# A two-layer flow-matching backbone on one core: one transfer issued earlier, eight half products left out, the end of a projection dealt out anew, and head sums as four small products

## The reference

```
h   = rms_norm(x) * (1 + scale) + shift          # latent and context tokens
u   = h @ w_in                                   # keys, values, decay and rate latents, receptances, gate
z   = token_shift(u)                             # three taps along the tokens
w   = exp(-exp(-softplus(-(w0 + tanh(wd) @ w2)) - 0.5));  a = sigmoid(a0 + ad @ a2)
kk  = k * k_k / max(norm_per_head(k * k_k), 1e-12)
for each direction, head, token:                 # state S is 64 x 64 per head, 16 heads
    S = S * w - (S kk) (kk a)^T + v k^T;   y = S r
bonus = sum_over_the_64_channels_of_a_head(r * k_dir * r_k) * v
o   = group_norm(y_0 + y_1) * gn_w + gn_b + bonus_0 + bonus_1
out = x + gate_l * ((o * silu(gate)) @ w_out)
```

## Time and profile before

| | us |
|---|---|
| timed runs, median (lowest to highest) | 4983.27 (4974.59 to 4983.56) |
| the profiled execution, its own time | 4975.48 |
| its span, first to last instruction | 4973.5 |
| end of the projection of layer 1 | 3051 |
| recurrence | 3051 to 4672 |
| output stage | 4672 to 4973 |

### The profile page before, as it was taken

One profiled execution on the slowest core, in us unless ns is written; L12 is line 12 of the kernel. 1 busy time (PEld: TensorE's weight loads), 2 busy tenths in 40 slices (PEclk: granted clock), 3 DMA queues, 4 the chain that ended last, 5 costly groups with the idle time before them and its releaser, 6 DMA issues. The chain is left out here.

```text
span 4973.5 us, 120092 instructions
## 1 busy us (share of the span) xinstructions
PE 4543.6 (91%) x48286; PEld 2711.2 (55%) x48286; DVE 2692.2 (54%) x4764; ACT 1699.0 (34%) x4125; POOL 1377.6 (28%) x2884
## 2 busy tenths in 40 slices
PE   6999996999999999899999996888988998989599
PEld 4666663333333333454444444777877877778444
DVE  2444443655666663222144444666766676666487
ACT  1222221444444443033122222444544555445232
POOL 1111111332322331000000001555555555555232
PEclk8999997999999999899999998999999999999799
DMA  5222223000000002632322334777776777776685
GB/s 215 94 88 95 85 77 127 4 25 24 25 25 24 25 6 100 224 137 102 117 67 80 95 99 135 177 192 177 179 179 175 180 187 188 178 181 162 175 261 173
DMA packets 994713, 603.89 MB, mean 121 GB/s; under 512 B 699045, under 2 KB 939173, under 8 KB 980136
## 3 DMA queue, kind: packets, MB, share of 16 engines
q1 hardware_dynamic: 907690, 574.11, 39.9%
q10 hardware_dynamic: 86528, 22.82, 2.2%
HBM read 390.44 MB, written 206.32 MB: 120 GB/s over the span
## 5 line engine op out<-in xcount | busy, mean ns | idle before, releaser
L934 PE MATMUL at_bS<-at_qT,at_kT 97*64 97x512 f32 (+1 forms) x2368 | 607.1, 598 | 15.1 <-ACT at_pT L1032 14.5
L1673 PE MATMUL p_bU<-keep_hT,p_slab 128*128 128x512 f32 (+1 forms) x1504 | 596.9, 554 | 13.5 <-DMA p_slab<-in_o_w_in_dram 7.4
L1069 DVE TENSOR_REDUCE at_mx<-at_bM 128x1 f32<-128x512 f32 (+1 forms) x656 | 394.0, 627 | 353.8 <-PE at_bM L899 352.8
L2321 PE MATMUL rw_bank<-keep_rw_hg,rw_slab 128*128 128x256 f32 x2048 | 493.0, 395 | 45.7 <-DMA keep_rw_hg<-scratch_hT 45.7
L1032 ACT ACTIVATE at_pT<-at_bS 128x512 f32<-128x512 f32 (+1 forms) x592 | 342.4, 591 | 398.3 <-PE at_bS L934 379.0
L2321 PEld LDWEIGHTS rw_bank<-keep_rw_hg,rw_slab 128*128 128x128 f32 x2048 | 390.8, 196 | 108.5 <-DMA keep_rw_hg<-scratch_hT 47.9
L1673 PEld LDWEIGHTS p_bU<-keep_hT,p_slab 128*128 128x128 f32 x1504 | 283.9, 191 | 297.8 <-issue 281.8
L2114 POOL TENSOR_TENSOR rw_g_at<-rw_g_at,rw_g_prod 64x14 f32<-64x14 f32 (+6 forms) x1008 | 328.4, 326 | 79.0
L856 POOL TENSOR_TENSOR at_sum_pool<-at_sum_pool,at_pT 128x512 f32<-128x512 f32 x192 | 243.9, 1270 | 372.3 <-ACT at_pT L1032 354.9
L2112 POOL TENSOR_TENSOR rw_g_prod<-rw_g_at 64x14 f32<-64x14 f32 (+6 forms) x1008 | 315.8, 313 | 79.1
L934 PEld LDWEIGHTS at_bS<-at_qT,at_kT 97*64 97x64 f32 x2368 | 155.4, 137 | 279.8 <-issue 187.6
(11 more groups left out here) (288 smaller groups left out, 9463.1 us busy)
## 6 DMA issues: line engine op xcount, KB each, us to landing
keep_rw_hg<-scratch_hT SPq DMA_DIRECT2D x64, 1024.0 KB
keep_wide<-scratch_heads SPq DMA_DIRECT2D x144, 384.0 KB, 4.3
keep_gate<-scratch_inverses SPq DMA_DIRECT2D x576, 64.0 KB
scratch_bq<-keep_wide SPq DMA_DIRECT2D x144, 128.0 KB, 2.5
scratch_products<-rw_NB SPq DMA_DIRECT2D x288, 64.0 KB
rw_Vt<-scratch_vt SPq DMA_DIRECT2D x144, 128.0 KB, 2.6
scratch_y<-rw_ysb ACTq DMA_DIRECT2D x288, 64.0 KB, 3.2
scratch_heads<-p_z SPq DMA_DIRECT2D x17, 1024.0 KB, 4.9
```

The source lines that it names most:

```text
L934: last = pe.matmul(bS[rows, g % 3, 0:nq * P], kT[:, s, k * P + VH * x:k * P + VH * x + VH], qT[:, s, q0 * P:(q0 + nq) * P], start=True, st ...
L1069: nc.vector.tensor_reduce(mx[:, j, piece:piece + 1], bM[:, (FIRST_ITEM[b] + i) % 2, 0:n], AX.X, ALU.max).then_inc(max_red, 1)
L1673: last = pe.matmul(bU[:, n % 4, 0:w], slab[:, i, k, :], hT[:, k, tok:tok + w], start=(k == 0), stop=(k == KD - 1))
L2321: last = pe.matmul(DENSE[:, GT * half:GT * (half + 1)], slab[:, half, q, :], hg[:, x.slot, q, :], start=(q == 0 and half == 0), stop=(q == ...
```

## The change

Four parts, all in layer 1.

1. *Recurrence, SP.* `dense_before(n)` moves up: it stood behind `keep_inverses` and `gather`, and now stands ahead of both, right behind `keep_products`. At the start of the stage, `low_rank` of the first body reads its latents from a free slot of the prefetch buffer (`zin[:, 1, i, 3]`), which the projection stage fills with two small loads; it no longer waits for `rw_lora`. The second body waits for two of the three parts.
2. *Recurrence, TensorE.* In the last pass `dense(x, 0)` returns after its waits: 8 bodies times 8 products fall away.
3. *End of the projection.* In the last pair the values' outer taps stand ahead of `p_kk` on VectorE; two of the five copies of the last values and two of their four stores go to ScalarE; and in every pair the stores of the values of the pair before stand ahead of the `p_kk` stores.
4. *Output stage.* A head sum is four products of 64 x 64 by 512 columns, one on each quarter of the array, in place of two of 128 x 128. For two of the quarters the bonus products of the second half of the head pairs are loaded with the two heads of a pair swapped, which takes three transfers in place of one for each direction. `turn` now stands ahead of `head_sums` on TensorE and takes over its waits, and at the start of the stage GpSimd's first power stands ahead of its first sum.

```
@@ projection, SP, every pair
                         if i == 0:
+                            if not (isinstance(p, int) and p == 0):
+                                store_values(p - 1)
                             sp.wait_ge(kk_done, p + 1)
                             store(heads[:, 1, :], kk, kk_st)
                             sp.dma_start(heads[:, 2, 0:CTX], kk[:, 0:CTX]).then_inc(kk_st, 16)
-                            if not (isinstance(p, int) and p == 0):
-                                store_values(p - 1)
@@ projection, SP, end
+                for i in range(2):
+                    sp.dma_start(zin[:, 1, i, 3], W["lora"][i, :, 0:GT]).then_inc(keep["rw_wl_l"], 16)
...
                 pair(PAIRS - 1, False)
-                store_values(PAIRS - 1)
+                sp.wait_ge(vt_out, NS * (PAIRS - 1) + 3)
+                sp.wait_ge(vt_last, 2)
+                for h in range(2):
+                    sp.dma_start(turned_rows(PAIRS - 1, 0, h), vt[0:HP, :, HP * h:HP * h + HP]).then_inc(vt_st, 16)
@@ projection, ACT, end
+                a.wait_ge(vt_st, 16 * 4 * (PAIRS - 1))
+                for x in (1, 3):
+                    a.wait_ge(vt_mm, NS * (PAIRS - 1) + x + 1)
+                    nc.scalar.copy(vt[:, 4 * x:4 * x + 4, :].rearrange("p q c -> p (q c)"), bS[:, x, :]).then_inc(vt_last, 1)
+                a.wait_ge(vt_last, 2)
+                a.wait_ge(vt_out, NS * (PAIRS - 1) + 3)
+                for h in range(2):
+                    a.dma_start(turned_rows(PAIRS - 1, 1, h), vt[HP:P, :, HP * h:HP * h + HP]).then_inc(vt_st, 16)
@@ projection, DVE
+                    if p == PAIRS - 1:
+                        shift_taps(0, 0, slice(p + KD, p + KD + 1), 4 + 2 * p, links + 3)
                     v.wait_ge(dchain, links + 3)
...
-                    shift_taps(0, 0, slice(p + KD, p + KD + 1), 4 + 2 * p, links + 3)
-                for x in range(NS):
+                    if p < PAIRS - 1:
+                        shift_taps(0, 0, slice(p + KD, p + KD + 1), 4 + 2 * p, links + 3)
+                for x in range(0, NS, 2):
                     values_out(PAIRS - 1, x)
@@ recurrence, SP
                     keep_products(n.on(3), 1)
+                    dense_before(n)
                     keep_inverses(n.on(2))
                     gather(n.on(3))
-                    dense_before(n)
                     spread(n.on(2))
@@ recurrence, PE
-                    if m.n < 3:
-                        pe.wait_ge(lora_l[m.n], 16)
+                    for part in ((), (0, 1), (2,))[m.n] if m.n < 3 else ():
+                        pe.wait_ge(lora_l[part], 16)
...
-                                                 lora[rows, i, span(tokens(m, d), GT)], start=True, stop=True, skip_group_check=True)
+                                                 lora[rows, i, span(tokens(m, d), GT)] if m.n else zin[rows, 1, i, 3, :], start=True, stop=True, skip_group_check=True)
...
                         pe.wait_ge(dn_out, x.t)
+                        if not x.queries:
+                            return
@@ output, SP
-                        sp.dma_start(bin_[:, s, d], W["bq"][d, :, rows(t, CTX)].rearrange("(k p) t -> p k t", p=P)).then_inc(b_l[s], 16)
+                        sp.dma_start(bin_[:, s, d, 0:4], W["bq"][d, 0:4 * P, rows(t, CTX)].rearrange("(k p) t -> p k t", p=P)).then_inc(b_l[s], 16)
+                        for h in range(2):
+                            other = W["bq"][d, 4 * P:, rows(t, CTX)].rearrange("(k h c) t -> h c k t", h=2, c=HP)[1 - h]
+                            sp.dma_start(bin_[HP * h:HP * h + HP, s, d, 4:8], other).then_inc(b_l[s], 16)
@@ output, POOL, start of the stage
-                bonus(0, 0)
                 rstd(0)
+                bonus(0, 0)
                 rstd(1)
@@ output, PE
                 def turn(t, s):
+                    pe.wait_ge(bs_done, t + 1)
+                    pe.wait_ge(bv_done, t)
                     pe.wait_ge(yn_done, t + 1)
...
-                def head_sums(t):
-                    pe.wait_ge(bs_done, t + 1)
-                    pe.wait_ge(bv_done, t)
+                def head_sums():
                     for j in range(2):
-                        last = pe.matmul(bB[:, j, :], same[:], bsum[:, 4 * j:4 * j + 4, :].rearrange("p k t -> p (k t)"), start=True, stop=True)
+                        for h in range(2):
+                            rows_in, rows_out = (slice(HP * x, HP * x + HP) for x in (h, h ^ j))
+                            last = pe.matmul(bB[rows_out, j, :], same[rows_in, rows_in], bsum[rows_in, 4 * j:4 * j + 4, :].rearrange("p k t -> p (k t)"),
+                                             start=True, stop=True, skip_group_check=True)
                     last.then_inc(hs_mm, 1)
...
                     if next1:
-                        head_sums(t + 1)
                         turn(t + 1, 1 - s)
+                        head_sums()
                     pe.wait_ge(o_done, t + 1)
```

24 lines of the change are left out of this document (13 added, 11 removed).

## The result

| | before | changed |
|---|---|---|
| timed runs, median (lowest to highest), us | 4978.93 (4970.96 to 4983.56) | 5102.57 (5096.81 to 5109.36) |
| the profiled execution, its span | 4973.5 | 5095.0 |
| last reciprocal's end to the start of the recurrence | 29.5 | 25.1 |
| recurrence | 1621.4 | 1752.3 |
| output stage | 300.9 | 298.5 |

The ratio is 1.0251, with a 95% interval of 1.0229 to 1.0272: 124 us slower, where 4937 us, 42 under this median, was forecast. The two stages at the ends became shorter, by 4.4 and 2.4 us. The recurrence lost 131 us.

The account below looks back on a forecast made before the run. TensorE, busy 91% of the span, was taken to bound the kernel. Gains of 4.2 + 4 + 28 + 2 + 4.4 = 42.6 us gave 4932.9 from the profiled 4975.5, 4940.7 from the median; forecast 4937, range 4912 to 4966.

Parts of the forecast that it names:

- End of the projection: Projection's last pair: earlier transposes, copies and stores, some on a second queue, gain 4.2 us, bounds 2 and 6.
- Start of the recurrence: Recurrence's first bodies: early latents worth 0, since the slice's transfer limits; earlier slice issue gains 4 us later.
- The 4 us for the fourth body: Recurrence's fourth body: earlier slice issue wins 4 us of 3.81 waited plus 2.36 of longer products, bounds 0 and 6.
- The hoist in the other bodies: Recurrence bodies without new slabs: 1 MB ahead of inverses' store, gather and eight loads costs 0, as GpSimd has slack.
- Cost 0: Recurrence bodies without new slabs: the earlier slice costs nothing, GpSimd being busy only 28% of the span.
- the fourth rival: Recurrence: small transfers behind 1 MB land late, TensorE waits in every body, 68 us lost, 5000 us; chance 0.05.
- my "slower" rival: Same as the fourth rival: small transfers come late in every recurrence body, 5000 us; chance 0.05.
- The hoist at the boundaries: Recurrence's seven pass boundaries: slabs issued 3.6 us earlier win 4 us each, 28 in all, bounds 14 and 42.
- Last pass: Recurrence's last pass without half 0 of the dense products: 2 us gain, bounds 11 of gain and 9 of loss.
- Output stage: Output stage: head sums 1.09 us for 1.88, loop period stays; gain 4.4 us, mostly at the start, bounds 2 and 16.
- R3: Recurrence boundaries: the hoist does nothing because slabs also wait for their buffer; only the ends gain, 4969 us; chance 0.06.

Follow-up runs that it names:

- x1: Kernel before with only the hoist: `dense_before` ahead of `keep_inverses` and `gather` in every body; ratio 1.0239.
- x9: Kernel before with GpSimd's inversion made longer by computing seven of its products twice; ratio 1.0106.
- x11: Changed kernel with only the parts at the ends, the slice loaded behind `spread` for the body after next; ratio 1.0010 to the kernel before.
- x3: Changed kernel with `dense_before` early only in the seven bodies that need new slabs, at its old place elsewhere; ratio 1.0008 to the kernel before.
- x18: x1 with the gather and the inverses' store issued by GpSimd on its own queue; ratio 1.0222 to the kernel before.
- x10: Kernel before with four of the fourteen steps of GpSimd's inversion left out; ratio 0.9998.
- x14: x11 with four of the fourteen steps of GpSimd's inversion left out as well; ratio 0.9986 to the kernel before.
- x6: Kernel before with half 0 of the dense products not issued in the last pass; ratio 1.0006.
- x4: Kernel before with `dense_before` between `keep_inverses` and `gather`, so only the gather is behind the slice; ratio 1.0113.
- x15: Kernel before with the gather issued by GpSimd on its queue, just ahead of its inversion; ratio 1.0059.

## Why the prediction was wrong, point by point

- *End of the projection*, 4.2 us: right. From the last reciprocal's end to the next stage 29.4 to 29.7 us in thirteen traces with the old end, 25.1 to 25.5 in seven with the new one.
- *Start of the recurrence*, the latents: right. From the start of the stage to the first dense product there are 14.4 to 14.7 us in nineteen traces, with the early load and without it, and 17.2 in the changed kernel's own. The 4 us for the fourth body did not come: in x1 the wait for its slice is gone (3.81 before), but the next of the rows that stand once a body comes 81.2 us into the stage, where it came after 80.9.
- *The hoist in the other bodies, "Cost 0"*: this is the step that failed, with 119 us. I had priced it by GpSimd's slack, read from its 28% of the whole span. Over the six passes it is busy 644.33 of 1175.05 us, 55%, and its 7.2 us of waiting in each body were mostly no slack: 2.5 us more of work on GpSimd cost 53 us (x9). But this is not where the loss came from. I then argued against the fourth rival that the eight loads "lie behind the same bytes before and after". The loads do, but what they wait for, the inverses' store, had been ahead of the 1 MB and went behind it; its landing rose from 4.0 to 7.6 us. The loads began 8.8 us after the products' stores in place of 5.2. That is my "slower" rival, with 0.05: its mechanism, small transfers that come late for TensorE in each body, was right. Its price of 68 us was too small, because it gave the loads 5 us in hand: they came 3.7 us later, and each undisturbed body grew by 2.1 us (21.31 to 23.40), which over its 57 bodies is 119. So what they had in hand was less than 3.7 us. The waits of `far_p`, 67.9 us, are only a part of the loss, and TensorE's products took longer as well.
- *The hoist at the boundaries*, 28 us: wrong too. The wait for the slice did fall, from 32.4 to 9.0 us, but x11 takes all of it away and x3 keeps the hoist to these bodies, and neither is faster. In the changed kernel the body of group 0 takes 28.4 us, where 23 was forecast. A wait on TensorE was read as time that would be won. The three bodies around a boundary take 67.3 us before, 68.6 in x11 and 70.1 in x3, whichever of them waits.
- *Last pass*, 2 us of gain: not confirmed, its sign open; the products filled gaps, as argued.
- *Output stage*, 4.4 us: 2.4. The head sums took 1.09 us and `m_yn` still 3.37, and the loop kept its period to 0.1 us, as forecast. The gain is at the start: the first `m_yn` stands 14.7 us into the stage in place of 17.5, 2.8 won of the 3.6 forecast, and the last at 259.9 in place of 262.2, so the steady tiles added nothing. Over the traces the stage takes 300.4 to 302.2 with the old form and 297.7 to 299.1 with the new one.
- The rule of the Trainium skill that I weighed, "DMA: Bandwidth & Descriptors", section "Queues, rings and completion order", that each DMA engine takes up the descriptors of a queue in the order of the ring, pointed the right way, and I left it out of the sum. The order within one queue is not what decides for the inverses' store: in x18 it has another queue than the slice and lands after 7.3 us (7.6 behind it on the same queue), and the kernel is as slow.
- One rival's sum is off: that of R3 adds 2 us for the last pass, which everywhere else is a gain of 2. With it as a gain, R3 gives 4965.

What stays open: how the 21.3 us of a body in the kernel before could be made shorter. By the chain they are 82% TensorE's own instructions, which agrees with x10, x11 and x14, where less inversion and no wait for the slice gave next to nothing. But fewer products on TensorE in the last pass gave nothing either (x6), so the amount of its work alone does not set the length there. Open too is why the same products took longer in the changed kernel.

## What to carry to other kernels

Before a large load is moved earlier, list every small transfer that it passes, and for each whose landing another transfer or engine waits for, add the large one's time on the engines to that round trip, in every iteration and not only where the load was late. A wait on the busiest engine is worth its length only if the iterations around it don't absorb it: sum the bodies on both sides of it. An engine's idle time is slack only if what it waits for does not depend, around the ring, on its own result, and its busy share must be read in the stage in question and not over the whole span.

## What the runs showed of the hardware

- A 128 KB store issued behind 1 MB landed after 7.6 us in place of 4.0, behind 512 KB after 6.1, behind 128 KB after 4.4, and from another queue than the 1 MB after 7.3: the delay went with the bytes, not with the queue.
- With the hoist the gather's first issue on SP, the second behind the 1 MB, took 3.7 us on the mean in place of 0.4, and up to 7.0: the engine that issues was itself held, and with it everything behind it. With 512 KB ahead it took 2.1 on the mean, with an eighth 0.9. The store's issue between the two took 0.4. In x4, where the gather is the next issue behind the 1 MB but comes later after the products' stores, it took 0.5. What decides which issue is held is not shown.
- The same 27024 products kept TensorE busy for 1099.66 us in place of 1048.77 where it also waited more, at a granted clock of 0.95 in place of 0.97.
- GpSimd can issue the gather itself, two issues of 0.67 us, but the kernel before was 0.6% slower for it (x15).
